# A two-layer prompt and sample block: the first projection split into two halves of channels, and one ring place given to modulation chunks during the other projections

## The reference, cut to what matters

```python
def adaln(cvec, w, b):
    m = jax.nn.silu(cvec) @ w + b
    return [t[:, None, :] for t in jnp.split(m, 6, axis=-1)]
...
sh1, sc1, g1, sh2, sc2, g2 = adaln(c, ada_w[l], ada_b[l])
h = rmsnorm(xs, norm_mix[l]) * (1 + sc1) + sh1
...
p = h @ w_in
q_lat, kv_lat, k_rope, na_qkv = jnp.split(p, [Q_RANK, Q_RANK + KV_RANK, Q_RANK + KV_RANK + ROPE_DIM], axis=-1)
q = rmsnorm((rmsnorm(q_lat, q_norm) @ w_q_up).reshape(B, L, MLA_HEADS, QK_DIM), q_gain)
ckv = rmsnorm(kv_lat, kv_norm)
```

## Time and profile before

| | |
|---|---|
| median of 3 runs | 1285.13 us (1284.8 to 1286.57) |
| the profiled execution | 1279.75 us, of it 1278.0 us span from first to last instruction |
| PE busy | 1132.6 us, 89% |
| DVE, ACT, GpSimd (POOL) busy | 566.0, 264.1, 174.6 us |
| bytes moved | 314.19 MB, mean 246 GB/s |
| chain that ended last | PE 81%, DMA 5%, DVE 5% |

### The profile page before, as it was taken

How to read it: one execution, slowest core, us unless ns; L and a number is a source line. 1 busy time by engine, 2 the same in 40 slices (tenths; PEclk the granted TensorE clock), 3 DMA queues, 4 the chain that set the end, 5 groups by cost and what they waited for, 6 DMA issues and landing times.

```text
span 1278.0 us, 26178 instructions
## 1 busy us (share of the span) xinstructions
PE 1132.6 (89%) x9175; PEld 653.2 (51%) x9176; DVE 566.0 (44%) x1225; ACT 264.1 (21%) x644; POOL 174.6 (14%) x261
## 2 busy tenths in 40 slices
PE   4899968989768899999799999999996788999995
PEld 3554646654564445455555654344556444555543
DVE  0122444463353344444543334777554334444445
ACT  1111324440111112121322113121010211212121
POOL 1043210000012111111100001111001111111110
PEclk9899989999868899999899998998995889999998
DMA  9832499782586899999931321000139598996894
GB/s 317 307 118 77 166 343 384 252 289 90 202 341 265 357 423 422 422 422 421 326 115 67 93 73 66 1 1 0 48 117 398 207 361 370 396 384 275 321 424 177
DMA packets 82734, 314.19 MB, mean 246 GB/s; under 512 B 11160, under 2 KB 12097, under 8 KB 57321
## 3 DMA queue, kind: packets, MB, share of 16 engines
q1 hardware_dynamic: 77098, 298.66, 60.2%
q10 hardware_dynamic: 3616, 7.67, 1.5%
q0 software_dynamic: 1952, 6.90, 1.5%
HBM read 307.82 MB, written 5.39 MB: 245 GB/s over the span
## 4 chain that ended last, share of the span: by engine, by line
PE 81%; DMA 5%; DVE 5%; issue 4%; SPq 2%; ACT 2%; POOL 1%; POOLq 0%; ACTq 0%; DVEq 0%
PE banks L457 78%; DMA arena<-in_ada_b 3%; DVE arena L991 3%; SPq L1880 1%; DMA arena<-token_rows,arena 1%; PE banks L629 1%; POOL arena L1784 1%; SPq L1878 1%; DVE arena L1137 1%; DMA mod_rows<-arena 1%; ACT arena L1599 1%; ACT arena L1589 1%; PE banks L832 0%; PE banks L508 0%; ACT arena L1506 0%
## 5 line engine op out<-in xcount | busy, mean ns | idle before, releaser
L457 PE MATMUL banks<-arena 32*128 32x256 f32 (+10 forms) x8748 | 1082.3, 423 | 111.3 <-issue 37.7
L457 PEld LDWEIGHTS banks<-arena 128*32 128x32 f32 (+4 forms) x8748 | 605.5, 157 | 562.8 <-issue 401.0
L991 DVE TENSOR_TENSOR arena<-banks,arena 128x64 f32<-128x64 f32 (+3 forms) x282 | 113.2, 413 | 69.4 <-PE banks L457 63.6
L991 DVE TENSOR_TENSOR arena<-arena 128x384 f32<-128x384 f32 (+13 forms) x229 | 134.3, 592 | 4.4
L1256 DVE SCALAR_TENSOR_TENSOR arena<-arena 128x768 f32<-128x768 f32 x81 | 84.4, 1042 | 107.8 <-issue 105.5
L1633 ACT ACTIVATE arena<-banks 128x512 f32<-128x512 f32 x79 | 47.2, 597 | 235.1 <-PE banks L457 235.1
L1792 POOL TENSOR_TENSOR arena<-arena 128x256 f32<-128x256 f32 x81 | 59.4, 733 | 242.8 <-PE banks L457 242.8
L1266 DVE TENSOR_SCALAR arena<-arena 128x64 f32<-128x64 f32 x79 | 15.4, 195 | 173.5 <-ACT arena L1637 173.5
L1771 POOL TENSOR_SCALAR arena<-arena 128x8 f32<-128x8 f32 (+2 forms) x28 | 7.1, 254 | 367.7 <-ACT arena L1490 262.3
L1801 POOL COPY arena<-arena 128x256 f32 x79 | 32.8, 415 | 178.9 <-PE banks L457 159.7
L1356 DVE TENSOR_SCALAR arena<-arena 128x385 f32<-128x385 f32 x24 | 11.6, 482 | 82.4 <-ACT arena L1694 82.4
(11 more groups left out here) (150 smaller groups left out, 446.1 us busy)
## 6 DMA issues: line engine op xcount, KB each, us to landing
arena<-in_moe_w_gate SPq DMA_DIRECT2D x64, 1024.0 KB, 8.9
arena<-in_moe_w_up SPq DMA_DIRECT2D x64, 1024.0 KB, 11.3
arena<-in_moe_w_down SPq DMA_DIRECT2D x64, 1024.0 KB, 11.5
arena<-in_ada_w SPq DMA_DIRECT2D x24, 2048.0 KB
arena<-in_hy_w_in SPq DMA_DIRECT2D x6, 2048.0 KB
arena<-in_attn_w_in SPq DMA_DIRECT2D x3, 2048.0 KB
arena<-mod_rows SPq DMA_DIRECT2D x8, 512.0 KB, 10.1
arena<-in_attn_w_out SPq DMA_DIRECT2D x2, 2048.0 KB
```

Of the source, the lines that this page charges most:

```text
L457: return pe.matmul(out, lhsT, rhs, start=start, stop=stop, skip_group_check=True)
L991: return dve.tensor_tensor(o, p, q, op)
```

## The change

The first four chunks come in the order 0, 2, 1, 3, so that shift and scale of the lower 512 channels are there after two chunks, and `win` 0 is loaded between the pairs. The first projection runs its `qlat` matmuls over the lower four channel groups, then, as chunks 1 and 3 land, `kvr`, and at last all matmuls over the upper four. `kvr` of the three tiles shares one bank, which DVE zeroes ahead (`kv_zero`); their readers wait for the last tile. In each half ACT evicts tiles 0 and 2 and DVE tile 1. Loads of the table and of the tokens move from ACT's queue to the head of SP's; ACT squares the tokens before it issues the loads of the gains; POOL issues the loads of the caches after the third chunk is used.

The places are written out beside the items. c0 stands after the first projection, c1 after nq1, c2 to c5 at units 0 to 3, c6, c7, c8 after the three `nv`, c9 to c14 at units 5 to 10, c15 to c19 at pairs 2, 6, 10, 14, 18. Place 1 carries chunks alone from c0 to c8; from c9 on places 0 and 1 take turns, and c15 to out 1 take the places 2, 0, 1, 2, 0, 1, 2. The later ring items (`items1`) start at place 1 in place of 0.

```diff
-            return n % 3 if n < 9 else (n - 9) % 2 if n < 15 else (n + 2) % 3
+            return places[n]
...
-        turn_of = {c: i for i, c in enumerate([(0, n) for n in range(4)] + chunks)}
-        items0 = ([("ada", 0, n) for n in range(4)] + [("win", i) for i in range(4)] + [("up",)]
-                  + [("ada", l, n) for l, n in chunks]
-                  + [("out", 0), ("out", 1)])
+        first_chunks = [(0, 0), (0, 2), (0, 1), (0, 3)]
+        turn_of = {c: i for i, c in enumerate(first_chunks + chunks)}
+        ch = [("ada", l, n) for l, n in chunks]
+        early = ([(("ada", 0, 0), 0), (("ada", 0, 2), 1), (("win", 0), 2), (("ada", 0, 1), 0), (("ada", 0, 3), 1), (("win", 1), 0)]
+                 + [(ch[0], 1), (("win", 2), 2), (ch[1], 1), (ch[2], 1), (("win", 3), 0)] + [(c, 1) for c in ch[3:6]]
+                 + [(("up",), 2)] + [(c, 1) for c in ch[6:9]] + [(c, i % 2) for i, c in enumerate(ch[9:15])]
+                 + [(ch[15], 2), (ch[16], 0), (ch[17], 1), (ch[18], 2), (ch[19], 0), (("out", 0), 1), (("out", 1), 2)])
+        items0 = [k for k, _ in early]
         items1 = [("hyin", i) for i in range(6)] + [("w3",), ("hyout", 0), ("hyout", 1)]
         items = items0 + items1
+        places = [p for _, p in early] + [(1 + i) % 3 for i in range(len(items1))]
...
-        at_unit = {6 + n: c for n, c in enumerate(chunks[:7])}
-        at_pair = {int(1.9 * n) + 1: c for n, c in enumerate(chunks[7:])}
+        at_unit = {n: chunks[2 + n] for n in range(4)}
+        at_unit.update({5 + n: chunks[9 + n] for n in range(6)})
+        at_pair = {2 + 4 * n: c for n, c in enumerate(chunks[15:])}
...
-                n0 = arrived(("win", 0))
-                w = item(n0, KC, WIN0)
+                w = item(arrived(("win", 0)), KC, WIN0)
+
+                def half(kind, t, j):
+                    c0, c1 = (0, QR) if kind == "qlat" else (QR, WIN0)
+                    o = ps[:, place[kind, t], :]
+                    o = o[:, 0:QR] if kind == "qlat" else o[:, t * (WIN0 - QR):(t + 1) * (WIN0 - QR)]
+                    for k in range(4 * j, 4 * j + 4):
+                        last = mm(o, hT[:, k, t * P:(t + 1) * P], w[:, k, c0:c1], kind == "qlat" and k == 0, k == KC - 1)
+                    if j:
+                        close(last, kind, t)
+
                 for t in range(T):
-                    hT_ready(0, t)
-                    for kind, c0, c1 in (("qlat", 0, QR), ("kvr", QR, WIN0)):
-                        o = open_(pe, kind, t, [("lat", t)], 2 * t + (kind == "kvr"))
-                        for k in range(KC):
-                            last = mm(o[:, 0:c1 - c0], hT[:, k, t * P:(t + 1) * P], w[:, k, c0:c1], k == 0, k == KC - 1)
-                        close(last, kind, t)
+                    open_(pe, "qlat", t, [("lat", t)], 2 * t)
+                    name, i = evicted(0, t, 0)
+                    sig(name).at(pe, i)
+                    half("qlat", t, 0)
+                open_(pe, "kvr", 0, [("lat", t) for t in range(T)], 7)
+                place["kvr", 1] = place["kvr", 2] = 7
+                sig("kv_zero").at(pe, 0)
+                ada(0, 1, 6)
+                turn_row(0, 1)
+                half("kvr", 0, 0)
+                ada(0, 3, 6)
+                half("kvr", 1, 0)
+                turn_row(0, 3)
+                half("kvr", 2, 0)
+                for t in range(T):
+                    name, i = evicted(0, t, 1)
+                    sig(name).at(pe, i)
+                    half("qlat", t, 1)
+                    half("kvr", t, 1)
...
+                ada(*chunks[0], 6)
                 produce(*units[0])
                 produce(*units[1])
+                ada(*chunks[1], 7)
                 for n, (kind, t) in enumerate(units):
                     if n + 2 < len(units):
                         if units[n + 2] == ("q", 0):
                             for tt in range(T):
                                 produce("nv", tt)
+                                ada(*chunks[6 + tt], 7)
...
-            ada(0, 0, 1)
             scaled_transposes(0)
-            for n in range(1, 4):
-                ada(0, n, (n + 1) % 2)
-                turn_row(0, n - 1)
-            turn_row(0, 3)
+            for n in (0, 2):
+                ada(0, n, 6)
+                turn_row(0, n)
...
+                ada_row(chunks[0])
...
+                ada_row(chunks[1])
...
+                        if n == 4:
+                            for c in chunks[6:9]:
+                                ada_row(c)
...
-            ada_row((0, 0))
+            sig("gains").at(dve, 0)
+            sig("kv_zero").by(dve.memset(ps[:, 7, 0:T * (WIN0 - QR)], 0.0), 0)
             for t in range(T):
                 scaled(0, t)
-            sig("gains").at(dve, 0)
-            for n in range(1, 4):
-                ada_row((0, n))
-                columns(0, n - 1)
-            columns(0, 3)
-            for t in range(T):
-                modulated(0, t)
+            for j in range(2):
+                for n in (j, 2 + j):
+                    ada_row((0, n))
+                    columns(0, n)
+                modulated(0, 1, j)
...
+            def first_hT_out():
+                for j in range(2):
+                    sig("colT").at(act, 1 + 2 * j)
+                    for t in (0, 2):
+                        o = read(act, "hT", 2 * t + j)
+                        g = min(t, 1)
+                        for k in range(4 * j, 4 * j + 4):
+                            ins = act.activation(hT[:, k, t * P:(t + 1) * P], o[:, k % 4 * P:(k % 4 + 1) * P], ACT.Identity,
+                                                 bias=shift[:, k, g:g + 1], scale=slope[:, k, g:g + 1])
+                        sig("hT").by(ins, 2 * j + t // 2)
...
-            act.dma_start(tab, a["tab"][:, 0:TAB]).then_inc(in_const, 16)
-            act.dma_start(x[:, 0, :], a["x_prompt"].rearrange("b t d -> (b t) d")).then_inc(in_x, 16)
-            act.dma_start(x[:, 1:3, :], a["x_sample"].rearrange("b (t p) d -> p (b t) d", p=P)).then_inc(in_x, 16)
             act.wait_ge(in_c, 48)
             sig("cexp").by(act.activation(v(WORK + 16, 2, KC), v(WORK, 2, KC), ACT.Exp, scale=-1.0), 0)
+            squares(0)
...
+                sig("psum_ada").at(pool, 2)
                 pool.dma_start(V[:, 3, NAW:], a["cache_na_v"].rearrange("b a t h d -> (b a t) (h d)")).then_inc(in_ctxv, 16)
-                sig("psum_hT").at(pool, 5)
...
-            for k in items0[:5]:
+            sp.dma_start(tab, a["tab"][:, 0:TAB]).then_inc(in_const, 16)
+            sp.dma_start(x[:, 0, :], a["x_prompt"].rearrange("b t d -> (b t) d")).then_inc(in_x, 16)
+            sp.dma_start(x[:, 1:3, :], a["x_sample"].rearrange("b (t p) d -> p (b t) d", p=P)).then_inc(in_x, 16)
+            groups = {(l, n): (l, j) for l in range(2) for j, n in enumerate((5, 9, 11))}
+            for n, k in enumerate(items0):
                 load(k)
-            sig("cT").at(sp, 0)
-            if stage >= 1:
-                load(items0[5])
-                load(items0[6])
-                sp.dma_start(bias.rearrange("p a b c d -> p (a b c d)"), a["bias"]).then_inc(in_bias, 16)
-                load(items0[7])
-                load(items0[8])
-                groups = {(l, n): (l, j) for l in range(2) for j, n in enumerate((5, 9, 11))}
-                for k in items0[9:]:
-                    load(k)
-
-                    n = number[k] - 2
-                    if items[n][0] == "ada" and items[n][1:] in groups:
-                        store_mod(*groups[items[n][1:]])
-                        if items[n][1:] == (0, 5):
-                            load_gate(0, 0)
+                if k == ch[0]:
+                    sp.dma_start(bias.rearrange("p a b c d -> p (a b c d)"), a["bias"]).then_inc(in_bias, 16)
+                done = items0[max(n - 2, 0)]
+                if done[0] == "ada" and done[1:] in groups:
+                    store_mod(*groups[done[1:]])
+                    if done[1:] == (0, 5):
+                        load_gate(0, 0)
```

More of the change, by code:

```diff
@@ L200, in build @@
         in_turn("psum_latents", [("psum_qlat", 1), ("psum_kvr", 1)])
-        in_turn("set_up", [("cT", 1), ("gains", 1)], False)
+        in_turn("set_up", [("cT", 1), ("gains", 1), ("kv_zero", 1)], False)
         in_turn("act_latents", [("nv", 3), ("latT", 4)], False)
@@ L1019, in columns @@
             def columns(l, n):
-                o = read(dve, "colT", l * 4 + n)[:, 0:P].rearrange("p (g r) -> p g r", g=4)[:, :, 0:2]
+                o = read(dve, "colT", turned_row(l, n))[:, 0:P].rearrange("p (g r) -> p g r", g=4)[:, :, 0:2]
                 k = slice(n % 2 * 4, n % 2 * 4 + 4)
@@ L1030, in scaled, with modulated @@
                 sig("xdiag").by(dve.tensor_scalar(xdiag[:, t, :], ident, rstd[:, t:t + 1], None, ALU.mult), u // 2 * 3 + t)
-            def modulated(u, t):
-                sig("colT").at(dve, u // 2 * 4 + 3)
-                o = read(dve, "hT", (u * 3 + t) * 2 + 1)
+            def modulated(u, t, j=1):
```

(20 more changed lines are left out.)

30 lines of the change are left out of this document (18 added, 12 removed).

## The result

The changed kernel is slower: 1298.26 us median (1293.11 to 1309.54, 6 runs) against 1284.69 (1280.0 to 1286.57, 6 runs) of the kernel before, ratio 1.0152 with a 95% interval of 1.0113 to 1.019. Forecast were 1288.9 and a range of 1279 to 1297: the sign was right (a slower kernel had been given 0.44), the size was not: +3.8 us forecast, +13.6 between the medians, and +22.0 at the turned rows of the profiled execution. That execution is the longest of its six (1309.54, span 1307.7); up to the turned rows another one, further down, agrees with it within 4 us.

The account below looks back on a forecast made before the run. PE's order of work was taken to bound the kernel, its matmuls being 78% of the chain. The terms summed to +3.8 us, added to the median for 1288.9 us, range 1279 to 1297.

Parts of the forecast that it names:

- head: Up to the end of the first projection: loading halves ends it at 60.9 against 69.38, -8.5 us.
- chunks moved, waits removed: Units: eight more chunks before the pairs at 2.3 each, +18.4 us; old landing waits and half clock gone, -12.6.
- waits added: Units: chunks on one place, then two, land later than PE needs them, +10.9 us together.
- gate: Ahead of c3, issued behind the row stores and gate load: idle 9.5 us, then half clock, +11.8 in all.
- end of units: After c14 at unit 10, PE turns one unit and waits 2.6 us for k2: +2.4, between 0 and 4.
- pairs: Eight chunks fewer, -14.0 us; the landing wait ahead of c8 and its slow clock go too, -4.6.
- A: The forecast case: the head's gain is handed back at place 1 and the gate; 1284 to 1294 us, chance 0.50.
- lone loads: Units, place 1: a chunk loaded alone takes 8.48 us, so c2, c4, c5, c7 and c8 wait 1.2 to 1.7.
- steps without a chunk: Pairs: two in a row were not in the trace; over 3.6 us, the pairs give back less than 14.
- B: Units, c2 and c4 to c8: lone loads land within a projection, so faster, 1280 us; chance 0.30.
- C: Units: PE's clock falls after each short wait, six waits at 1.3 to 1.9 each, 1298 us; chance 0.10.
- D: Head: the halves don't start early, loads some 4 us later, the gain halves, 1293 us; chance 0.10.

Follow-up runs that it names:

- repeated: The changed kernel once more with no edit and a second profile; 1296.93 us, ratio 1.013 to the kernel before.
- cut chunks: Changed kernel with c7 to c14 cut on TensorE to 8 of their 36 calls; first scores 217.28, turned rows 307.11 us, median not used.
- the run with the gate late: Changed kernel with the gate's load issued behind out 1 and not ahead of c3; 1295.79 us, ratio 1.0125; once more, 1286.81, ratio 1.0058.
- filling the waits: Changed kernel with idle matmuls ahead of nine landing waits and four meant for k2's turn, results overwritten; 1292.94 us, ratio 1.0087.
- the run of the places alone: Kernel before with its old head, but the new places, positions and order from c0 on; 1306.29 us, ratio 1.0222.

## Why the prediction was right in sign and wrong in size

| term of the sum | predicted | profile after | repeated |
|---|---|---|---|
| head | -8.5 | -5.4 | -6.2 |
| chunks moved, waits removed | +5.8 | taken as +5.8 | taken as +5.8 |
| waits added, their slow clock in | +10.9 | +17.6 | +15.9 |
| gate, its slow clock in | +11.8 | +11.1 | +11.8 |
| end of units | +2.4 | +2.7 | +2.3 |
| pairs | -18.6 | -12.7 | -15.1 |
| not assigned | | +2.9 | +3.9 |
| turned rows | +3.8 | +22.0 | +18.4 |

The measured waits are the sums of the brackets on `in_ada_b` without c3's, plus what c6, c13 and c14 took over 2.31 (9.37 with a tile); the gate's is c3's idle plus what c3 took over 2.31. "Not assigned" is what is left of the mark. 1.5 and 2.5 of it are a half clock that the sum didn't hold: in the first profile the turns of k2, k3 and the cache took 1.36, 1.94 and 1.09 where 1.12, 1.12 and 0.63 are full; in the repeated run the turns from k1 on lost 1.6 and the turn and the projection behind c3 0.9. Some 1.4 us in both stay open.

**Confirmed.** The mechanism of A: the head's gain is handed back at place 1 and at the gate. c3's idle of 9.68 against 9.5 and the wait of 2.66 ahead of k2 against 2.6 came almost as worked out, the gate's partly by luck: on the clock of this run c3 was issued 1.4 later than I had it, the stores taking 7.9 us from their issue where I counted 5.6 from the landing of c2, and it was used 11.5 after its issue and not 12.6. The lone loads came out too: c2, c4, c5, c7 and c8 wait 1.21 to 1.50 against 1.2 to 1.7. The steps without a chunk take 3.2 us, under the 3.6 that I named as the limit, and a chunk's price in the pairs held (below).

**The step that failed is the sum, in three of its terms, all to the same side, and in the half clock behind k2's wait, which it put at nothing (1.5 us above).**

*Waits added, +10.9.* c6 behind `up` waited 3.14 and then ran at the half clock (2.0 forecast, no clock). For c12 to c14 I took 1.6 in all from bytes against cadence (5.3 against 5.0 is only 0.3 a load); it was 1.70 and 3.08 with 1.3 of clock. The cut chunks show why: this stretch is bound by landings, 5.3 us being near the shortest interval there (5.2 to 5.8) and not the mean one. A queue that runs at its limit can't be costed by its mean.

*The pairs, -14.0 and -4.6.* Together -12.7 and -15.1 in the two executions. The price of a chunk held. In the middle, from 221.38 to here,

```profile
282.34 0.85 PE L629 MATMUL banks<-arena 128*128 128x128 f32 x6 [1.60 <-ACT arena L1599]
```

the old kernel takes 60.96 us with eight chunks, the changed one 51.27 with three (252.09 to 303.36), the repeated run 50.62: 1.9 and 2.1 for each of five, where I had 1.95 and 1.55. What failed is the clock at both ends. To 221.38 the old takes 28.74; I had 8.5 less (two chunks and the landing term), and it was 4.1 and 5.8. The slow clock that I let go with c8 came back at the scores and c15: 2.08 where 1.16 is full, and 4.93 for 76 instructions, 2.95 in the run with the gate late. By that 2.95, c8's 4.24 held 1.3 of slow clock and not the 1.9 in my -4.6. Behind 282.34 the old takes 8.53; with a chunk less both new executions take 9.5, at the half clock behind the wait of 1.88.

*The head, -8.5.* The windows show it, as the earlier trace rows:

```profile
30.00:32.00 2.00, 0.00 (x0) 0.00 (x0) 0.00 (x0) 1.16 (x4) 0.00 (x0) 0.50 1.05 396
30.00:40.00 10.00, 7.84 (x15) 4.37 (x16) 0.00 (x0) 1.16 (x4) 0.00 (x0) 0.59 0.85 320
40.00:50.00 10.00, 9.50 (x167) 6.97 (x166) 0.75 (x3) 0.00 (x0) 2.44 (x4) 1.00 0.33 104
```

`win` 0 landed at 32.16, not 30.5 (30.19 to 32.41 over the nine profiles with this head). The rate wasn't lower up to there, 396 GB/s; by the windows 10.5 MB had moved at 32 us, 1.8 more than I had ahead of `win` 0, where the same count gives 0.9 more in the old head. Which bytes went ahead isn't shown. After 4.1 us of idle the lower `qlat` ran at a granted clock of 0.59: 10.9 us (13.19 less a chunk's 2.31) where I had 9.6. In the last window the DMA engines are two thirds idle: chunk 3 was no longer what PE waited for, but the upper halves began 2.7 late all the same, at 52.66.

**The rivals.** B fell: a lone chunk takes 8.67 from issue to use. The Trainium skill's fit (DMA: Bandwidth & Descriptors, Anatomy of one DMA), made for DMAs that GpSimd issues and estimated at 6.8 for a chunk, is below every one of these landings; by it the waits wouldn't be there. C fell in its form: after 1.2 to 1.7 us of waiting the next chunk takes 2.30 or 2.31, the full clock, and filling the waits gave 1.1 us. But the half clock did follow waits of 1.88 (late in the pairs), 1.99 (c14, repeated run, 3.49) and 2.83 to 3.14 (c6), and after less busy units it lasted 20 us; in the run of the places alone it followed neither 2.02 (c13) nor 2.77 (c6). The Trainium skill (TensorE: Matmul & The Clock Gate, HAM oscillation) shows bursts of matmuls that start cold between waits for loads of some 3 to 5 us; here the half clock came behind shorter waits too, and not behind each. D is half true: the halves start early, and 3 us of the gain were not there.

What stays open is the gate's size in the median (1 or 9 us), half of the old kernel's gain from a later gate, what the half clock behind k2's wait and at the end of the pairs would give back, and the 1.4 us that no term holds.

## What to carry to other kernels

A ring place that carries one kind of load can deliver one per issue, landing and use; here 8.6 us and 2.3, which fits between projections of 7 us only at every second one. Before a load moves into a stretch without gaps, ask what it costs there (2.3 us of PE and any wait) and what it gives back where it was (1.9 in the middle of the pairs); then look at what PE's clock does where PE has less to do. A store with a load that depends on it belongs behind the last load of that queue that somebody waits for; and when a sum of many opposite terms is near zero, its small terms deserve their upper bounds in the range together.

## What the runs showed of the hardware

Runs of one kernel on one chip differ by more than most edits here: 29 of the old one lay between 1268.95 and 1290.65 us, with spans from 1267.2 us at a mean granted clock of 0.943 to 1288.9 at 0.923. Marks inside the kernel vary less: turned rows of the same change at 309.25 and 312.91.

A chunk issued 5.0 us behind another was used 12.6 us after its issue (9.6 in the repeated run), a lone one after 8.67. From the issue of the stores of c0 and c1 to that of the load that waits for them SP took 7.9 us in both kernels. And TensorE kept the half clock from 220 to 240 us while busy without a gap, after the thinned units; with whole chunks in the units those two windows were granted 0.74 and 0.92 in the repeated run.
